# Homes outside the expert ring for the gate sigmoids and the gated part, and three expert chunks sent for during mixing

## The reference, cut to what matters

```python
def hybrid_layer(x, ...):
    h = rms_norm(x, norm1_gain)
    p = h @ w_in
    q, k, v, p_rwkv, p_gate = jnp.split(p, ...)
    y_att = att.reshape(B, S, ATT_OUT_WIDTH) @ w_att_out      # windowed attention
    y_rwkv = rwkv7_time_mix(p_rwkv, ...)                      # recurrence, ends in @ w_rwkv_out
    gates = jax.nn.sigmoid(p_gate)
    mixed = gates[..., :D] * y_att + gates[..., D:] * y_rwkv
    x = x + mixed @ w_out
    x = x + hierarchical_moe(rms_norm(x, norm2_gain), ...)    # 32 experts, top 2
    return x

def hierarchical_moe(h, ...):
    # group softmax, top group, top 2 experts in it; for each expert, on its tokens:
    hid = jax.nn.silu(xb @ w_expert_gate[e]) * (xb @ w_expert_up[e])
    return hid @ w_expert_down[e]
```

## Time and profile before

| | |
|---|---|
| median of three runs | 1358.11 us |
| the profiled execution's own time | 1356.83 us |
| its span | 1355.0 us |
| TensorE busy | 1160.0 us, 86% |
| VectorE busy | 737.7 us, 54% |
| ScalarE busy | 487.1 us, 36% |
| chain that ended last | PE 66%, DMA 17%, DVE 3% |
| read from HBM | 346.93 MB |
| mixing's output products begin | 259.96 us |
| experts' first products begin | 299.76 us |

### The profile page before, as it was taken

The page is one execution under the profiler, slowest core; times in us unless marked ns, Lnnn a source line. Parts: engine busy times, 40 slices in busy tenths (PEclk is TensorE's granted clock), DMA queues, the critical chain, the costliest instruction groups (busy, mean ns, idle before and its releaser), DMA issues.

```text
span 1355.0 us, 22776 instructions
## 1 busy us (share of the span) xinstructions
PE 1160.0 (86%) x9669; PEld 919.5 (68%) x9669; DVE 737.7 (54%) x1120; ACT 487.1 (36%) x657; POOL 2.6 (0%) x11
## 2 busy tenths in 40 slices
PE   7999989997657366564739999999999999999998
PEld 6998778973213121221314998999998998999997
DVE  5487655852101010010104898877777899877776
ACT  4543435330000000000004546644446556644444
POOL 0000000000000000000000000000000000000000
PEclk9999999998878697788869999999999999999999
DMA  8842225999999999999999646566655436566650
GB/s 270 281 149 63 65 80 210 342 405 416 426 427 424 428 427 424 429 426 427 426 419 361 212 149 179 160 201 186 187 156 179 156 127 181 172 189 187 187 156 31
DMA packets 180986, 349.52 MB, mean 258 GB/s; under 512 B 8140, under 2 KB 154737, under 8 KB 167954
## 3 DMA queue, kind: packets, MB, share of 16 engines
q1 hardware_dynamic: 180394, 347.40, 70.6%
q10 hardware_dynamic: 488, 0.62, 0.2%
HBM read 346.93 MB, written 3.43 MB: 259 GB/s over the span
## 4 chain that ended last, share of the span: by engine, by line
PE 66%; DMA 17%; DVE 3%; issue 2%; SPq 1%; ACT 1%; DVEq 1%; ACTq 0%
PE ps L2868 25%; PE ps L2904 12%; DMA expert_ring<-in_w_expert_up 7%; PE ps L2058 6%; DMA expert_top<-in_w_expert_up 4%; PE ps L2089 4%; DMA expert_early<-in_w_expert_up 2%; DMA expert_ring<-in_w_expert_gate 2%; PE ps L225 2%; PE ps L2046 2%; PE ps L1708 2%; PE ps L2103 2%; PE ps L254 2%; PE ps L2880 2%; PE ps L2842 2%
## 5 line engine op out<-in xcount | busy, mean ns | idle before, releaser
L3216 DVE TENSOR_TENSOR w_lo<-expert_early,w_hi 128x2048 fp32r<-128x2048 f32 x80 | 182.8, 2291 | 25.7 <-ACT w_hi L3010 22.9
L2058 PE MATMUL ps<-expert_ring,w_slot 128*32 128x512 f32 x640 | 113.6, 712 | 96.7 <-DMA expert_ring<-in_w_expert_gate 40.9
L2131 DVE TENSOR_TENSOR hT<-ps,hT 128x512 f32<-128x512 f32 x8 | 8.5, 1068 | 340.9 <-PE ps L2058 340.9
L3010 ACT ACTIVATE w_hi<-expert_early 128x2048 fp32r<-128x2048 f32 x80 | 153.0, 1918 | 56.5 <-PE ps L2904 34.1
L2058 PEld LDWEIGHTS ps<-expert_ring,w_slot 128*32 128x32 f32 x640 | 30.3, 129 | 159.5 <-issue 159.5
L2868 PE MATMUL ps<-x_hi,w_hi 128*128 128x256 f32 x960 | 134.2, 282 | 0.0
L2868 PE MATMUL ps<-x_hi,w_lo 128*128 128x256 f32 x960 | 134.1, 282 | 0.0
L2868 PE MATMUL ps<-x_lo,w_hi 128*128 128x256 f32 x960 | 132.3, 280 | 0.0
L2868 PEld LDWEIGHTS ps<-x_hi,w_hi 128*128 128x128 f32 x960 | 122.9, 188 | 3.8 <-issue 1.6
L2868 PEld LDWEIGHTS ps<-x_hi,w_lo 128*128 128x128 f32 x960 | 123.0, 190 | 0.0
L2868 PEld LDWEIGHTS ps<-x_lo,w_hi 128*128 128x128 f32 x960 | 121.0, 188 | 0.0
(11 more groups left out here) (531 smaller groups left out, 2095.5 us busy)
## 6 DMA issues: line engine op xcount, KB each, us to landing
expert_ring<-in_w_expert_gate SPq DMA_DIRECT2D x22, 2048.0 KB, 29.4
expert_ring<-in_w_expert_up SPq DMA_DIRECT2D x18, 2048.0 KB, 29.3
expert_early<-in_ffn_up SPq DMA_DIRECT2D x36, 1024.0 KB, 6.0
expert_ring<-in_w_expert_down SPq DMA_DIRECT2D x14, 2048.0 KB, 29.8
w_slot<-in_w_in SPq DMA_DIRECT2D x26, 1024.0 KB, 5.5
expert_early<-in_w_in SPq DMA_DIRECT2D x20, 1024.0 KB, 5.5
expert_early<-in_ffn_down SPq DMA_DIRECT2D x18, 1024.0 KB, 4.9
expert_early<-in_w_expert_gate SPq DMA_DIRECT2D x6, 2048.0 KB, 26.9
```

The costliest lines, as they stand in the source:

```text
L2058: mm = pe.matmul(m.ps[rows_of(e), b, :], x_quad[:, k, rows_of(e)], w[e][:, k, :], start=(k == 0), stop=(k == KC - 1))
L3010: act.activation(w_hi[:, half_slot(l, i), :], raw_slot(m, i), ACT.Copy).then_inc(S["w_hi"], 1)
L3216: dve.tensor_tensor(w_lo[:, s, :], raw_slot(m, i), w_hi[:, s, :].bitcast(F32), ALU.subtract).then_inc(S["w_lo"], 1)
```

## The change

The eight pairs of sigmoids leave the ring: the first four go to `w_up`, `a_up` and the two halves of `g_up`, the last four to `hT`, which the gate products have finished reading by then. The recurrence's half of a gated product goes to the first half of `o_T` instead of `gate_part`. With slot 3 free from the end of the recurrence, chunk 3 is sent right behind chunk 2. Chunk 4 (slot 4) is sent once the last branch product is made, APART once two of the four gated parts are, both in the loop over w_out's pieces, ahead of the last piece.

```diff
@@ -930,7 +930,7 @@
     v_room, q_room, g_room, s_room = (sb(n, [P, 8, P]) for n in ("v_tok", "q_T", "g_bd", "state"))
     assert sb.at == m.ring_at + 56 * KB
     rate = sb("rate", [P, 8, P])
-    sig_first = sb("sig_first", [P, 2, 2, SEQ])
+    sb.at += 4 * KB
     from_beta, from_kappa = squares("from_beta", 2), squares("from_kappa", 2)
     sq, sq_t, q4, x_t, n1 = (squares(n)[:, :, 0, :] for n in ("sq", "sq_t", "q4", "x_t", "n1"))
     w_inv = sb("w_inv", [P, 8, P])
@@ -945,9 +945,9 @@
 
     def pair(x):
         return x.rearrange("p (c t) -> p c t", c=2)
-    rate_sig = rate[:, :, :].rearrange("p (g f) n -> p g (f n)", g=2)
-    m.sig = [sig_first[:, 0, :, :], sig_first[:, 1, :, :], pair(m.w_up[:, :]), pair(m.a_up[:, :]),
-             pair(m.g_up[:, 0, :]), pair(m.g_up[:, 1, :]), pair(rate_sig[:, 0, :]), pair(rate_sig[:, 1, :])]
+    h_sig = m.hT[:, :, :].rearrange("p (g c) t -> p g c t", c=2)
+    m.sig = [pair(m.w_up[:, :]), pair(m.a_up[:, :]), pair(m.g_up[:, 0, :]), pair(m.g_up[:, 1, :])
+             ] + [h_sig[:, g, :, :] for g in range(GATES - WHOLE)]
 
     kk, kk_sq = beta_room[:, 0:8, :], beta_room[:, 8:16, :]
     kk_inv = kappa_room[:, 0:8, :]
@@ -1621,7 +1621,7 @@
     assert room.at <= m.ring_at
     room = Room(nc, m.ring_at + 64 * KB)
     branch_hi, branch_lo = room("branch_hi", [P, 6, SEQ], F32R), room("branch_lo", [P, 6, SEQ], F32R)
-    part = room("gate_part", [P, 2, SEQ])
+    part = m.o_T[:, 0:2, :]
     room = Room(nc, m.ring_at + 80 * KB)
     w_pair = room("w3_pair", [P, SPLITS, 2, 2 * D], F32R)
     w_hi, w_lo = w_pair[:, :, 0, :], w_pair[:, :, 1, :]
@@ -1659,6 +1659,7 @@
         sp.wait_ge(m.gate_lo, 4)
         load_mix_piece(sp, m, a, 2)
         load_expert_chunk(sp, m, a, 2)
+        load_expert_chunk(sp, m, a, 3)
         load_rows(sp, m, a, 0)
         sp.wait_ge(branch_lo_done, 2)
         for name, c0, c1 in (("group", 0, 4), ("expert", 4, NL)):
@@ -1673,14 +1674,18 @@
             if i == RING + 1:
                 sp.wait_ge(m.gate_done, 2 * GATES)
                 load_expert_chunk(sp, m, a, TOP)
+            if i == RING + 2:
+                await_filled(sp, ("rwkv", 3))
+                load_expert_chunk(sp, m, a, 4)
+                sp.wait_ge(gated, 2)
+                load_expert_chunk(sp, m, a, APART)
+
         def load_extra_row(f):
 
             src = a["w_expert_down"][0, CHUNKS[EXTRA][1]].rearrange("(p c) n -> p c n", p=P)
             sp.dma_start(m.extra_rows[f], src[:, f, :]).then_inc(m.first_rows[f], 16)
 
-        for g in (3, 4, APART, 5, 6, 7):
-            if g == 3:
-                sp.wait_ge(gated, 4)
+        for g in (5, 6, 7):
             if g == 5:
                 await_filled(sp, ("out", 2, 1))
             if g == 6:
```

## The result

The changed kernel takes 1368.47 us (median of six runs, 1367.54 to 1369.21) against 1358.41 us (six runs, 1356.71 to 1358.75): ratio 1.0075, 95% interval 1.0063 to 1.0087, 10.1 us slower. The forecast was 1367.5. The profiled execution took 1368.67 us with a span of 1366.9.

What follows compares the result with a forecast made beforehand. Transfers were taken to set the pace, TensorE following. A TensorE delay of 8.3 + 1.7 = 10.0 us made chunk 7 land 9.4 late; 1356.83 + 9.4 = 1366.2, from the median 1358.11 1367.5, range 1361.0 to 1370.0.

Steps and rivals of the forecast that it cites:

- piece 3 lands later: Output weight's first quarter, held behind the early chunk 3, lands at 260.6 instead of 255.7.
- output products i = 1 later: Mixing: the end of TensorE's first output product comes 2.1 us later, through DVE's late low part.
- piece 6 lands later: Output weight's last piece, behind 4 MB of chunk 4 and APART, lands at 285.8 instead of 270.9.
- clock behind the stop: After TensorE's 5.2 us stop before the last output product, matmuls partly run at the lower clock: 1.7 us more.
- chunk 7 lands later: Last chunk sent for before the experts begin lands at 314.3 instead of 304.9, +9.4 us.
- The slack: Before the last output product: TensorE waits for nothing if piece 6 lands by 277.2.
- The next piece swallows it: Mixing: some 3 us of delay from pieces 3 and 5 vanish behind the later piece 6.
- The hole: Low traffic at 245 to 255 us, 192 and 222 GB/s, is moved, not filled, by the early chunk 3.
- The rival that counts on up to 5 us of idle queue: Chunk 3 fills the low-traffic window, pieces come up to 5 us earlier: 1361.1 to 1363.1 us, chance 0.11.
- From chunk 7 on: Expert stage: the queue is full again, so the stage and all after it move by 9.4 us.
- Out of order: Rival: piece 6 passes the 4 MB and lands 9.8 us earlier, at 276.0; 1360.5 us, chance 0.04.
- Not slower: Rival: piece 6 lands by 277.2, TensorE waits for nothing, at most -0.9 us; 1357.2 us, chance 0.05.

Runs made afterwards that it cites:

- homes: Changed kernel with chunk 3, chunk 4 and APART sent in the old order, keeping only the new tiles for sigmoids and gated part: 1358.29 us, ratio 1.0003.
- c3_early: Changed kernel with chunk 4 and APART sent behind piece 6, chunk 3 still early: 1362.74 us, ratio 1.0037 to the kernel before.
- c4_ahead: Changed kernel with chunk 3 sent behind piece 6, chunk 4 and APART still ahead of it: 1363.48 us, ratio 1.0042 to the kernel before.
- reordered: Changed kernel with chunk 3 and piece 3 ahead of all router transfers, TOP behind piece 5, chunk 4 and APART behind piece 6: 1358.31 us, ratio 0.9999.
- fill: Changed kernel with chunk 3 between the group router's bias and expert router's weight, chunk 4 and APART behind piece 6: 1361.85 us, ratio 1.0037.

## Why the prediction was right

The time was 1.0 us off, and the steps came out as follows, each on its own count, in the first pair of profiles and in the second.

| step | forecast | measured | second pair |
|---|---|---|---|
| homes | 0 | 0 (homes) | |
| piece 3 lands later | 4.9 | 5.1 | 4.6 |
| output products i = 1 later | 2.1 | 3.8 | 1.9 |
| piece 6 lands later | 14.9 | 14.6 | 14.7 |
| product i = 3 begins later | 8.3 | 8.1 | 8.2 |
| clock behind the stop | 1.7 | 2.3 | 2.0 |
| experts begin later | 10.0 | 10.6 | 10.2 |
| chunk 7 lands later | 9.4 | 9.3 | 9.3 |
| the whole, by the medians | 9.4 | 10.1 | |

*The change part by part.* The decisive step, chunks 4 and APART ahead of piece 6, is shown by c3_early, which takes them away, and c4_ahead, which has them alone. The slack, 277.2 as the last harmless landing, is borne out from both sides: 275.5 costs nothing, 281.2 costs 5.1 us. "The next piece swallows it" holds for the 3 us that pieces 3 and 5 cost, and should not be read of chunk 3 as a whole: its 4.9 us of queue also make piece 6 later, as the sum had it, and half of the loss goes with them.

*The output products.* The stop ahead of the first one was forecast at 2.6 us and came at 2.8 and 2.4. What was put at nothing is the clock behind it. In the first profile the first six matmuls, from 262.23, take 1.62 us where they took 0.98, and product i = 1 is 3.8 us late; in the second the clock stayed up, and it is 1.9 us late, near the 2.1 forecast.

*The clock.* The last product's 24 matmuls take 5.3 us where they take 3.0 elsewhere: 2.3, and 2.0 in the second profile, not 1.7. The size was taken from a pair of stops in another stage, whose matmuls are of another shape. That it came out so near is in part luck, since stops of like length did not always bring the lower clock.

*The hole.* The forecast had it moved, not filled, and that came out; but the reason given, SP being held by a queue without room, is not what makes it so. In reordered piece 3 was sent at 240.7, ahead of all stops, and the same bytes were in no sooner. The rival that counts on up to 5 us of idle queue had nothing to stand on: fill and reordered show that no time is free in those ten microseconds.

*From chunk 7 on.* This is the step that was argued wrongly. I let all behind it move by chunk 7's 9.4, on the ground that the queue is full from there. By the traffic behind chunk 7 it is not, until chunk 12, whose issue waits for TensorE; that issue moved by 10.6 and 10.2 us, and the whole by 10.1. In c3_early, too, chunk 7 lands only 1.8 us later, the experts begin 3.3 later, and the time is 4.4 longer (3.1 to 6.8). By these rows it is the delay of the experts' start that is carried on. The forecast came near because here the two delays differ by only about a microsecond.

*Rivals.* Out of order: on SP's queue the landings came in the order of issue, and from a second queue piece 6 was in no sooner than the end of the 4 MB. Not slower: reordered is that case, with all pieces inside their slack but for 0.2 us ahead of the first output product, and no gain shows; one of the 0.9 us given as its cap is too small to tell. None of the orders tried gave a gain clear of the noise.

## What to carry to other kernels

Where one queue is full, sending a load earlier only makes another one later: write down the slack of each transfer that something waits for, and put ahead of it no more bytes than its slack times the rate (4.9 us for 2 MB here). Before moving loads forward, ask what the last of them waits for; if the issues that end the stage hang on an engine's work, bytes landed sooner buy nothing, and delay to that engine's operands is paid in full. A window with little traffic need not be an idle queue when its transfers have short rows: find out what would fit in by trying. The DMA share did not tell it either; it was 0.75 and 0.68 where no room was.

## What the runs showed of the hardware

- A 1 MB transfer with rows of 1 KB, on ACT's queue, took 19.6 us to land beside 4 MB and more of long rows on SP's; alone behind an emptying queue such a piece lands in 5.3.
- The stretch of the router's and the vectors' short rows, at 192 to 222 GB/s, had no room: chunk 3 put among them delayed what came behind by 5.2 us, as if no time had been free.
- SP can be held for 6.6 to 10.3 us by the issue of a transfer of 2 KB, and for 5.4 us by that of a chunk of 2 MB. The end of the stop at the router's bias moved by 5.4 us with a chunk put ahead of it, and by 3.0 with eleven small transfers taken away.
- Stops of TensorE of 2.0, 2.5 and 2.8 us were followed by the lower clock on the next six matmuls (1.32, 1.62 and 1.62 us), others of 2.4 and 2.9 us were not (0.96 and 0.96). The length of such a stop does not decide by itself. Behind 4.2 us the next 24 matmuls took 2.3 us more, behind 5.6 us 2.0.
